# A hybrid pooling/HGRN2 trunk in float32: weights stored tile by tile, loaded a megabyte at a time

## The chip, the core and the metric

The kernel runs on one core of a Trainium2 chip. The metric is device time in microseconds (us), from launch to end, and lower is better. Batch 1, 256 tokens, model width 2048, two layers, all data float32. Each weight is read once, so some 570 MB come from HBM in every execution.

## The reference, cut to what matters

```python
def reference(x, c, ...):
    cond = silu(c)
    for layer in range(2):
        mod = cond @ w_ada[layer] + b_ada[layer]              # 2048 x 12288, a vector times a matrix
        sh_m, sc_m, g_m, sh_f, sc_f, g_f = split(mod, 6)
        h = rms_norm(x, norm_mix_gain[layer]) * (1 + sc_m) + sh_m
        if layer == 0: y = pool_mixer(h, pool_w[0], pool_scale[0])   # four 512 x 512 products
        else:          y = hgrn2_mixer(h, hgrn_w_in[0], ...)         # 2048 x 8192 and 2048 x 2048
        x = x + g_m * y
        h = rms_norm(x, norm_ffn_gain[layer]) * (1 + sc_f) + sh_f
        x = x + g_f * swiglu(h, w_ffn_in[layer], w_ffn_out[layer])   # 2048 x 11264 and 5632 x 2048
    return rms_norm(x, final_gain)
```

## The kernel before

**Dense weights.** Every dense product is split in two parts for accuracy. A weight pair is 2 x 128 rows by 512 columns (512 KB). SyncE loads it into one of four places of the ring `raw` (`load_w`, line 381). ScalarE rounds it into `w_hi` (line 940), VectorE takes the rest, `w_lo = raw - w_hi` (line 1273), and TensorE runs six matmuls for each of the pair's two steps of 128 rows (lines 613 to 615, twelve a pair). `w_hi` and `w_lo` have four places too (`SPL`). Three semaphores tie this together: `hi(n)` waits until pair n has arrived and until TensorE has used pair n - 4. The load of pair n waits for `lo_ready` to reach n - 3, that is for `w_lo` of pair n - 4. TensorE waits for `lo_ready`.

**Modulation.** The vector `mod` is made in units of 1024 columns, sixteen tiles of 128 rows by 1024 columns (512 KB) each. There are 24 units. The first seven (`HEAD`) come before the feed-forward part of layer 0, and there the ring of tiles has sixteen places (`ada` and `ada_head`). Within a unit of the head the first 6 to 9 tiles go to TensorE (`multiply_loads`, line 641), and the others are folded by VectorE (`fold`, lines 1319 and 1322), which before its last fold adds TensorE's part (line 1316). TensorE then sums over partitions (line 648, or 675 for gates), ScalarE takes the result (lines 966 to 973), and only then can TensorE begin the loads of the next unit, since `modp` is one buffer. The seventh unit (`MIX_F`) takes 512 columns from each of two sections.

The other 17 units (`BEHIND`) run beside the dense products, all sixteen tiles on VectorE, through four places (`ada`). Each has a span of steps in which its tiles fall due.

**Order.** There is no scheduler: SyncE, ScalarE and VectorE each walk through the same list of steps (one step is 128 rows of a weight chunk), and at each step do what falls due. SyncE at step s issues the raw load of that step's pair (when s is even) and then the modulation tiles due at s. ScalarE and VectorE do `hi` or `lo` of that pair at step s, then the evacuations and updates of earlier chunks, then the folds due at s. All queues are in order, so a wait in one instruction holds back all behind it. Layer 0's feed-forward input begins with chunks of only four steps (36 chunks), in whose second half VectorE also adds each chunk to a partial sum (`add_quarter`, line 1618), and TensorE waits for that before it reuses a `prod` buffer (`evacuated`).

The weights lie in HBM as given: a raw pair is 256 rows of 2048 bytes, a modulation tile 128 rows of 4096 bytes (the seventh and the eighth unit 256 rows of 2048).

Of the kernel before, what the change touches and what calls it, by code (L numbers as in the profile page):

```python
# [14 lines left out]
P = 128  # L15
CH = 512
# [23 lines left out]
    return [k for k in range(n) if first + k * (last - first + 1) // n == step]  # L40


def build(nc, x, c, norm_mix_gain, norm_ffn_gain, w_ada, b_ada, pool_w, pool_scale, hgrn_w_in,
          hgrn_w_out, hgrn_norm_gain, hgrn_lb, w_ffn_in, w_ffn_out, final_gain, out):
    D = x.shape[2]
    TB = x.shape[1] // P
    S = TB * P
    KD = D // P
    NCH = D // CH
    F = w_ffn_out.shape[1]  # L50
    KF = F // P
    NF = F // CH
    HG = CH // P
# [117 lines left out]
    with ctx:  # L171
# [3 lines left out]
        def sem(name):  # L175
            return ctx.enter_context(nc.semaphore(name))
# [87 lines left out]

        C_GMIX, C_GFFN, C_HGAIN, C_LB = KD, 3 * KD, 5 * KD, 6 * KD

        raw_loaded = [sem(f"raw_loaded{i}") for i in range(RAW)]
        ada_loaded = [sem(f"ada_loaded{i}") for i in range(ADA_HEAD)]
        ada_free = [sem(f"ada_free{i}") for i in range(ADA_HEAD)]
        params_loaded = sem("params_loaded")  # L270
# [81 lines left out]
        def ada_buffer(slot):  # L352
            return ada[:, slot] if slot < ADA else ada_head[:, slot - ADA]

        def ada_arrived(eng, n):
            slot, before = ada_slot(n)
            eng.wait_ge(ada_loaded[slot], 16 * (before + 1))

        def ada_used(eng, n):
# [12 lines left out]
        @block.sync  # L372
        def _(sp):
            t = Tally()

            def load_w(src):
                n = t.get("raw")
                slot = n % RAW
                if n >= RAW:
                    sp.wait_ge(lo_ready, n - RAW + 1)  # L380
                sp.dma_start(raw[:, slot], src.rearrange("(a p) n -> p a n", p=P)).then_inc(raw_loaded[slot], 16)  # L381
                t.tick("raw")

            def load_ada():
                u, k = t.get("ada") // KD, t.get("ada") % KD
                layer, section, half = UNITS[u]
                mixed = section == MIX_F
                at = SH_F * D + half * CH if mixed else section * D + half * UW
                if k == ADA and not in_columns(u):
                    n = rows_before(u)  # L390
                    if n > 1:
                        sp.wait_ge(unit_summed, 2 * (n - 1))
                    for r in range(2):
                        row = 64 * (n % 2) + 32 * r
                        col = at + r * (D if mixed else CH)
                        sp.dma_start(bias[row:row + 1, :], b_ada[layer:layer + 1, col:col + CH]).then_inc(bias_loaded[n % 2], 16)
                slot, before = ada_slot(t.get("ada"))
                if before:
                    sp.wait_ge(ada_free[slot], before)
                block = w_ada[layer, k * P:(k + 1) * P]  # L400
                if mixed:
                    block = block[:, SH_F * D:(SC_F + 1) * D].rearrange("p (a d) -> p a d", a=2)[:, :, half * CH:(half + 1) * CH]
                    into = ada_buffer(slot).rearrange("p (a n) -> p a n", a=2)
                    sp.dma_start(into, block).then_inc(ada_loaded[slot], 16)  # L404
                else:
                    sp.dma_start(ada_buffer(slot), block[:, at:at + UW]).then_inc(ada_loaded[slot], 16)  # L406
                t.tick("ada")

            def load_unit(first=0, last=KD):
                for _ in range(first, last):  # L410
                    load_ada()

            def load_chunk(src, at, first, n, loaded=0):
                for s in range(n):
                    if s % 2 == 0 and s >= loaded:
                        k = first + s
                        load_w(src[k * P:(k + 2) * P, at:at + CH])
                    for span in SPAN.values():
                        for _ in due(t.get("step"), KD, *span):
                            load_ada()  # L420
                    t.tick("step")

            at = 0
            for src in (c, norm_mix_gain, norm_ffn_gain, hgrn_norm_gain, hgrn_lb):
                n = src.shape[0] * KD
                sp.dma_start(rows[at:at + n, :], src.rearrange("l (k p) -> (l k) p", p=P)).then_inc(params_loaded, 16)
                at += n
            load_unit(0, ADA)
            for n, section in enumerate((SH_M, SH_F)):
                sp.dma_start(brows[2 * n * KD:2 * (n + 1) * KD, :],  # L430
                             b_ada[0, section * D:(section + 2) * D].rearrange("(k p) -> k p", p=P)).then_inc(brows_loaded, 16)
            load_unit(ADA, KD)
            for tb in range(TB):
                sp.dma_start(xs[:, tb], x[0, tb * P:(tb + 1) * P, :]).then_inc(x_loaded, 16)
            load_unit()
            load_unit()
            load_chunk(pool_w[0, 0], 0, 0, HG)
            load_unit()
            load_chunk(pool_w[0, 1], 0, 0, HG)
            load_unit()  # L440
            load_chunk(pool_w[0, 2], 0, 0, HG)
            load_chunk(pool_w[0, 3], 0, 0, HG)
            sp.dma_start(pscale[:, :, :].rearrange("p a n -> p (a n)"),
                         pool_scale[0:1, :].to_broadcast([P, D])).then_inc(pscale_loaded, 16)
            load_unit()
            for s in range(0, AHEAD, 2):
                load_w(w_ffn_in[0, s * P:(s + 2) * P, 0:CH])
            load_unit()

            def load_ffn_in(layer):  # L450
                for first, n in ((0, HALF), (HALF, HALF)) if layer else ((0, HG), (HG, HG), (HALF, HALF)):
                    for j in range(NA):
                        for o in range(2):
                            load_chunk(w_ffn_in[layer], o * F + j * CH, first, n, 0 if layer or first or j or o else AHEAD)
                for j in range(NA, NF):
                    for o in range(2):
                        load_chunk(w_ffn_in[layer], o * F + j * CH, 0, KD)

            load_ffn_in(0)
            for n in range(NCH):  # L460
                load_chunk(w_ffn_out[0], n * CH, 0, KF)
            load_chunk(hgrn_w_in[0], D, 0, KD)
            load_chunk(hgrn_w_in[0], 0, 0, KD)
            for i in range(NCH):
                load_chunk(hgrn_w_in[0], i * CH + 2 * D, 0, KD)
                load_chunk(hgrn_w_in[0], i * CH + 3 * D, 0, KD)
                if i + 1 < NCH:
                    load_chunk(hgrn_w_in[0], i * CH + (D + CH), 0, KD)
                    load_chunk(hgrn_w_in[0], i * CH + CH, 0, KD)
            for first, n in ((0, WFIRST), (WFIRST, HG)):  # L470
                for half in range(2):
                    load_chunk(hgrn_w_out[0], half * CH, first, n)
            for n in range(2, NCH):
                load_chunk(hgrn_w_out[0], n * CH, 0, KD)
            load_ffn_in(1)
            for n in range(NCH):
                if n == NCH - 1:
                    assert t.get("ada") == KD * len(UNITS)
                    for slot in range(2):
                        ada_used(sp, t.get("ada") - ADA + slot)  # L480
                    sp.dma_start(fgain, final_gain.rearrange("(a n) -> a n", a=1).to_broadcast([P, D])).then_inc(fgain_loaded, 16)
                load_chunk(w_ffn_out[1], n * CH, 0, KF)
            last = D - CH
            sp.wait_ge(y_ready, 1)
            sp.dma_start(out[0, 0:P, last:], xs[:, 0, last:]).then_inc(stored, 16)
            sp.wait_ge(y_block, 1)
            sp.dma_start(out[0, 0:P, 0:last], xs[:, 0, 0:last]).then_inc(stored, 16)
            sp.wait_ge(y_ready, 2)
            sp.dma_start(out[0, P:S, CH:], xs[:, 1, CH:]).then_inc(stored, 16)
            sp.wait_ge(y_block, 2)  # L490
            sp.dma_start(out[0, P:S, 0:CH], xs[:, 1, 0:CH]).then_inc(stored, 16)
            sp.wait_ge(stored, 16 * 4)
# [438 lines left out]
        def _(act):  # L931
            t = Tally()

            def hi():
                n = t.get("pair")
                r, slot = n % RAW, n % SPL
                act.wait_ge(raw_loaded[r], 16 * (n // RAW + 1))
                if n >= SPL:
                    act.wait_ge(w_used, n - SPL + 1)
                act.activation(w_hi[:, slot], raw[:, r], ACT.Copy).then_inc(hi_ready, 1)  # L940
# [325 lines left out]
        def _(dve):  # L1266
# [636 lines left out]

_NAMES = ["x", "c", "norm_mix_gain", "norm_ffn_gain", "w_ada", "b_ada", "pool_w", "pool_scale", "hgrn_w_in",
          "hgrn_w_out", "hgrn_norm_gain", "hgrn_lb", "w_ffn_in", "w_ffn_out", "final_gain"]


# [14 lines left out]
```

## Time and profile before

| | us |
|---|---|
| median of 3 runs | 2180.79 (2180.61 to 2182.24) |
| the profiled execution | 2180.74 |
| its span, first to last instruction | 2179.0 |
| TensorE busy in the span | 2129.1 (98%) |
| VectorE busy | 1641.3 (75%) |
| ScalarE busy | 998.5 (46%) |
| moved by DMA | 574.34 MB, mean 264 GB/s |

The span is read in three parts. The head, up to 180 us, makes the first seven modulation units and the pooling mixer, and there the DMA queue is full all the time. From 180 to about 400 us the first chunks of the feed-forward part run with modulation tiles beside them, and VectorE is busy nearly all the time. The rest is dense products with TensorE at 97 to 100% of nearly every slice. "PE" is TensorE, "PEld" its weight loads, "DVE" VectorE, "ACT" ScalarE, "SPq" the queue of SyncE.

### The profile page before, as it was taken

To read this page: it belongs to the slowest core of one execution; us is meant where nothing else is said; L and a number is where in the kernel's file an instruction comes from. 1 tells how busy PE (TensorE), PEld (TensorE's weight loads), DVE (VectorE), ACT (ScalarE), POOL (GpSimd) and SP (SyncE) were. 2 spreads that over 40 slices of the span, in tenths; PEclk is the share of its full clock that TensorE was granted. 3 is DMA by queue.
4 is the path that set the end of the run, shared out by engine and by line. 5 is a ranking of instruction groups with operands and counts; after the bars stand their busy time and mean duration, and the time that the engine had idled before them with its cause. 6 is when DMAs were issued, how large, how long until landed. Compare 5 with 4: busy or idle time off the path is not lost.

```text
span 2179.0 us, 24643 instructions
## 1 busy us (share of the span) xinstructions
PE 2129.1 (98%) x9513; PEld 1724.2 (79%) x9513; DVE 1641.3 (75%) x1685; ACT 998.5 (46%) x1116; POOL 21.0 (1%) x89
## 2 busy tenths in 40 slices
PE   7999999999999999999999999999999999999997
PEld 3556887888888888878888888878888888888886
DVE  5778899999988887769787887677755665546644
ACT  3224544444444344455655556544454444444433
POOL 1000000000000000020000000000000000000000
PEclk9999999999999999999999999999999999999999
DMA  9999998999899998757666765578866666658663
GB/s 375 406 400 356 334 349 290 323 319 316 313 337 328 348 331 289 260 175 232 220 197 216 224 196 163 186 281 303 280 185 189 185 182 189 192 188 299 234 216 135
DMA packets 250353, 574.34 MB, mean 264 GB/s; under 512 B 17558, under 2 KB 17750, under 8 KB 249724
## 3 DMA queue, kind: packets, MB, share of 16 engines
q1 hardware_dynamic: 250236, 572.77, 77.2%
q8 instruction: 75, 1.23, 0.2%
q14 instruction: 42, 0.34, 0.0%
HBM read 570.60 MB, written 2.10 MB: 263 GB/s over the span
## 4 chain that ended last, share of the span: by engine, by line
PE 89%; DVE 4%; SPq 3%; DMA 2%; issue 2%; ACT 0%; ACTq 0%; DVEq 0%
PE prod L613 28%; PE prod L615 27%; PE prod L614 27%; PE small L684 1%; DVE acc L1322 1%; SPq L406 1%; DMA ada_head<-in_w_ada 1%; PE modp L641 1%; PE small L856 1%; SPq L404 1%; DMA pscale<-in_pool_scale 1%; SPq L381 1%; PE small L831 0%; PE modp L675 0%; DVE feat L1322 0%
## 5 line engine op out<-in xcount | busy, mean ns | idle before, releaser
L940 ACT ACTIVATE w_hi<-raw 128x1024 fp32r<-128x1024 f32 x696 | 736.4, 1061 | 992.8 <-PE prod L615 892.7
L1273 DVE TENSOR_TENSOR w_lo<-raw,w_hi 128x1024 fp32r<-128x1024 f32 x696 | 848.8, 1223 | 419.7 <-ACT w_hi L940 418.1
L613 PE MATMUL prod<-w_hi,h_hi 128*128 128x512 f32 x2072 | 819.3, 395 | 4.8 <-issue 1.9
L615 PE MATMUL prod<-w_hi,h_lo 128*128 128x512 f32 x2072 | 808.9, 390 | 0.0
L614 PE MATMUL prod<-w_lo,h_hi 128*128 128x512 f32 x2072 | 808.5, 390 | 0.0
L613 PEld LDWEIGHTS prod<-w_hi,h_hi 128*128 128x128 f32 x2072 | 390.3, 188 | 86.6 <-issue 3.2
L615 PEld LDWEIGHTS prod<-w_hi,h_lo 128*128 128x128 f32 x2072 | 389.7, 188 | 81.7
L614 PEld LDWEIGHTS prod<-w_lo,h_hi 128*128 128x128 f32 x2072 | 390.3, 188 | 78.7 <-issue 1.0
L1322 DVE SCALAR_TENSOR_TENSOR acc<-ada,cond,acc 128x1024 f32<-128x1024 f32 x255 | 326.4, 1280 | 0.4
L613 PE MATMUL prod<-w_hi,g_hi 128*128 128x512 f32 x688 | 269.1, 391 | 0.0
L615 PE MATMUL prod<-w_hi,g_lo 128*128 128x512 f32 x688 | 268.0, 390 | 0.0
L614 PE MATMUL prod<-w_lo,g_hi 128*128 128x512 f32 x688 | 267.9, 389 | 0.0
L614 PEld LDWEIGHTS prod<-w_lo,g_hi 128*128 128x128 f32 x688 | 129.2, 188 | 27.2 <-issue 0.5
L613 PEld LDWEIGHTS prod<-w_hi,g_hi 128*128 128x128 f32 x688 | 129.2, 188 | 27.2 <-issue 0.5
L615 PEld LDWEIGHTS prod<-w_hi,g_lo 128*128 128x128 f32 x688 | 129.2, 188 | 26.7
L641 PE MATMUL modp<-ada,cond_rows 128*128 128x512 f32 x112 | 56.4, 662 | 12.3 <-DMA brows<-in_b_ada 6.8
L641 PEld LDWEIGHTS modp<-ada,cond_rows 128*128 128x128 f32 x112 | 23.5, 215 | 41.9 <-issue 39.0
L684 PE MATMUL small<-ident,tok 128*128 128x128 f32 x272 | 37.4, 282 | 7.0 <-issue 4.8
L684 PEld LDWEIGHTS small<-ident,tok 128*128 128x128 f32 x272 | 32.8, 145 | 13.8 <-issue 6.9
L641 PE MATMUL modp<-ada_head,cond_rows 128*128 128x512 f32 x96 | 42.3, 592 | 0.0
L1322 DVE SCALAR_TENSOR_TENSOR acc<-ada_head,cond,acc 128x1024 f32<-128x1024 f32 x29 | 37.2, 1284 | 3.7 <-DMA ada_head<-in_w_ada 1.4
L1022 ACT ACTIVATE feat<-small,mod,gain 128x256 f32<-128x256 f32 x48 | 23.4, 563 | 29.2 <-PE small L684 26.7
(196 smaller groups left out, 1052.5 us busy)
## 6 DMA issues: line engine op xcount, KB each, us to landing
raw<-in_w_ffn_in SPq DMA_DIRECT2D x352, 512.0 KB, 4.6
ada<-in_w_ada SPq DMA_DIRECT2D x300, 512.0 KB, 6.2
raw<-in_w_ffn_out SPq DMA_DIRECT2D x176, 512.0 KB, 4.7
raw<-in_hgrn_w_in SPq DMA_DIRECT2D x128, 512.0 KB, 3.9
ada_head<-in_w_ada SPq DMA_DIRECT2D x84, 512.0 KB, 14.8
raw<-in_hgrn_w_out SPq DMA_DIRECT2D x32, 512.0 KB, 3.8
raw<-in_pool_w SPq DMA_DIRECT2D x8, 512.0 KB, 15.6
xs<-in_x SPq DMA_DIRECT2D x2, 1024.0 KB, 17.0
```

The lines of the kernel that those rows point to most:

```text
L381: sp.dma_start(raw[:, slot], src.rearrange("(a p) n -> p a n", p=P)).then_inc(raw_loaded[slot], 16)
L404: sp.dma_start(into, block).then_inc(ada_loaded[slot], 16)
L406: sp.dma_start(ada_buffer(slot), block[:, at:at + UW]).then_inc(ada_loaded[slot], 16)
L613: pe.matmul(o, hi[:, k, ts], wh, start=(begin and s == 0), stop=False)
L614: pe.matmul(o, hi[:, k, ts], wl, start=False, stop=False)
L615: mm = pe.matmul(o, lo[:, k, ts], wh, start=False, stop=(end and s == n - 1))
L641: mm = pe.matmul(modp[:, o], cond_rows[:, k], ada_buffer(slot)[:, o * CH:(o + 1) * CH], start=(k == 0), stop=(in_columns(u) and k == n_row ...
L684: mm = pe.transpose(small[half][:, o:o + P], block_of(tb, 2 * half + j), ident[:, :])
L940: act.activation(w_hi[:, slot], raw[:, r], ACT.Copy).then_inc(hi_ready, 1)
L1022: ins = act.activation(feat[:, half, j], small[half][:, j * S:(j + 1) * S], ACT.Identity, bias=shifts[:, k:k + 1], scale=gains[:, k:k + 1])
L1273: dve.tensor_tensor(w_lo[:, slot], raw[:, r], w_hi[:, slot], ALU.subtract).then_inc(lo_ready, 1)
L1322: ins = dve.scalar_tensor_tensor(a, ada_buffer(slot), cond[:, k:k + 1], a, ALU.mult, ALU.add)
```

## The change

Three things, all about how weights lie in HBM and how they are loaded. No arithmetic of the program changes.

- Before the launch, dense weights are stored tile by tile (`weight_tiles`): a tile is 512 rows by 512 columns, laid so that each of 128 partitions has its four row pieces, 8192 bytes, in one run. The tile is 1 MB in one piece. The modulation weights are stored as pairs of tiles (`modulation_tiles`), 8192 bytes a partition, and the mixed units lie ready in an array of their own.
- `load_w` loads such a tile, two pairs, with one DMA into two neighbouring places of `raw`. It waits for `lo_ready` to reach n - 2 (n even), that is for `w_lo` of pair n - 3. `raw_loaded` has two semaphores instead of four, and `hi` of either pair waits for the whole tile.
- In the head `load_ada` loads two modulation tiles with one DMA, once both places are free, and every user of either tile waits for both. Behind the head it still loads one tile at a time, in rows of 4096 bytes.

```diff
+def weight_tiles(w):
+
+    lead, (K, N) = w.shape[:-2], w.shape[-2:]
+    n = len(lead)
+    w = w.reshape(*lead, K // (4 * P), 4, P, N // CH, CH)
+    return w.transpose(*range(n), n + 3, n, n + 2, n + 1, n + 4).reshape(*lead, N // CH, K // (4 * P), P, 4 * CH)
+
+
+def modulation_tiles(w):
+
+    L, D, _ = w.shape
+    sections = w.reshape(L, D // (2 * P), 2, P, 6, 2, D // 2).transpose(0, 4, 5, 1, 3, 2, 6)
+    mixed = w[0, :, 3 * D:5 * D].reshape(D // (2 * P), 2, P, 2, D // CH, CH)[:, :, :, :, 0:2].transpose(4, 0, 2, 1, 3, 5)
+    return sections, mixed.reshape(2, D // (2 * P), P, 2, 2 * CH)
...
-        raw_loaded = [sem(f"raw_loaded{i}") for i in range(RAW)]
+        raw_loaded = [sem(f"raw_loaded{i}") for i in range(RAW // 2)]
...
         def ada_arrived(eng, n):
+
             slot, before = ada_slot(n)
+            if n < len(HEAD) * KD:
+                slot -= slot % 2
+            elif slot % 2:
+                before -= len(HEAD) * KD // ADA_HEAD
             eng.wait_ge(ada_loaded[slot], 16 * (before + 1))
...
                 if n >= RAW:
-                    sp.wait_ge(lo_ready, n - RAW + 1)
-                sp.dma_start(raw[:, slot], src.rearrange("(a p) n -> p a n", p=P)).then_inc(raw_loaded[slot], 16)
-                t.tick("raw")
+                    sp.wait_ge(lo_ready, n - RAW + 2)
+                sp.dma_start(raw[:, slot:slot + 2].rearrange("p b a n -> p (b a n)"), src).then_inc(raw_loaded[slot // 2], 16)
+                t.tick("raw", 2)
...
                 slot, before = ada_slot(t.get("ada"))
-                if before:
+                tiles = ada_mixed[half] if mixed else ada_sections[layer, section, half]
+                if u >= len(HEAD):
                     sp.wait_ge(ada_free[slot], before)
-                block = w_ada[layer, k * P:(k + 1) * P]
...
-                    sp.dma_start(ada_buffer(slot), block[:, at:at + UW]).then_inc(ada_loaded[slot], 16)
+                    sp.dma_start(ada_buffer(slot), tiles[k // 2, :, k % 2]).then_inc(ada_loaded[slot], 16)
+                elif k % 2 == 0:
+                    for tile in range(2 if before else 0):
+                        sp.wait_ge(ada_free[slot + tile], before)
+                    sp.dma_start(ada_pair(slot).rearrange("p k n -> p (k n)"),
+                                 tiles[k // 2].rearrange("p k n -> p (k n)")).then_inc(ada_loaded[slot], 16)
                 t.tick("ada")
...
-                    if s % 2 == 0 and s >= loaded:
+                    if s % 4 == 0 and s >= loaded:
                         k = first + s
-                        load_w(src[k * P:(k + 2) * P, at:at + CH])
+                        load_w(src[at // CH, k // 4])
...
-                act.wait_ge(raw_loaded[r], 16 * (n // RAW + 1))
+                act.wait_ge(raw_loaded[r // 2], 16 * (n // RAW + 1))
```

## Rows read from the trace of the kernel before

**Rows 1.** The page: span, busy time of the engines.
```profile
span 2179.0 us, 24643 instructions
...
PE 2129.1 (98%) x9513; PEld 1724.2 (79%) x9513; DVE 1641.3 (75%) x1685; ACT 998.5 (46%) x1116; POOL 21.0 (1%) x89
```

**Rows 2.** Stretches: length, busy of five engines, PEclk, DMA share, GB/s.
```profile
12.00:16.00 4.00, 4.00 (x7) 1.70 (x7) 0.00 (x0) 0.00 (x0) 0.00 (x0) 1.00 1.03 412
26.00:28.00 2.00, 0.00 (x0) 0.00 (x0) 1.91 (x2) 0.00 (x0) 0.00 (x0) 1.00 1.04 430
26.00:31.00 5.00, 1.69 (x8) 1.59 (x8) 4.87 (x5) 0.00 (x0) 0.00 (x0) 0.74 1.00 415
...
146.00:154.00 8.00, 8.00 (x37) 6.64 (x36) 5.85 (x6) 0.00 (x0) 0.00 (x0) 1.00 1.04 387
...
310.00:335.00 25.00, 23.21 (x100) 18.21 (x99) 24.80 (x24) 9.38 (x9) 0.00 (x0) 1.00 0.83 281
360.00:378.00 18.00, 16.87 (x77) 13.36 (x77) 17.93 (x18) 8.07 (x10) 0.00 (x0) 1.00 0.77 271
```

**Rows 3.** Who waited for whom: total us, times, longest.
```profile
SPq L381 <- DVE w_lo L1273: 1513.4, 677, 16.8
...
ACT w_hi L940 <- PE prod L615: 892.7, 573, 4.4
...
PE prod L613 <- DVE part_value L1618: 1.8, 2, 1.6
...
PE prod L613 <- DVE part_gate L1618: 1.1, 2, 0.7
```

**Rows 4.** Timeline, the head: start, us, engine, line, operation [idle before].
```profile
16.41 0.76 DVE L1319 TENSOR_SCALAR acc<-ada_head,cond 128x1024 f32<-128x1024 f32 x1 [7.12 <-DMA ada_head<-in_w_ada]
17.62 9.62 DVE L1322 SCALAR_TENSOR_TENSOR acc<-ada_head,cond,acc 128x1024 f32<-128x1024 f32 x7 [0.45 <-DMA ada_head<-in_w_ada]
...
125.53 1.02 ACT L966 ACTIVATE gate<-modp 128x1024 f32<-128x1024 f32 x1 [23.02 <-PE modp L675]
...
129.40 2.81 PE L641 MATMUL modp<-ada,cond_rows 128*128 128x512 f32 x6 [3.90 <-DMA ada<-in_w_ada]
```

**Rows 5.** Timeline, one pair in the steady state, on ScalarE, VectorE and SyncE.
```profile
719.15 1.06 ACT L940 ACTIVATE w_hi<-raw 128x1024 fp32r<-128x1024 f32 x1 [1.66 <-PE prod L615]
721.88 1.06 ACT L940 ACTIVATE w_hi<-raw 128x1024 fp32r<-128x1024 f32 x1 [1.66 <-PE prod L615]
...
720.25 1.23 DVE L1273 TENSOR_TENSOR w_lo<-raw,w_hi 128x1024 fp32r<-128x1024 f32 x1 [0.30 <-ACT w_hi L940]
...
721.50 0.37 SPq L381 DMA_DIRECT2D raw<-in_w_ffn_out  x1
```

**Rows 6.** The tile raw, 1000 to 1300 us: issue to landing of its loads.
```profile
DMA to landing us min/median/max: 3.6/3.9/6.8
```

**Rows 7.** DMA issues, 188 to 225 us: count, size, median us to landing.
```profile
raw<-in_w_ffn_in SPq DMA_DIRECT2D x13, 512.0 KB, 8.3
```

**Rows 8.** Timeline of VectorE, 258 to 358 us.
```profile
264.92 1.22 DVE L1273 TENSOR_TENSOR w_lo<-raw,w_hi 128x1024 fp32r<-128x1024 f32 x1
...
271.92 1.22 DVE L1273 TENSOR_TENSOR w_lo<-raw,w_hi 128x1024 fp32r<-128x1024 f32 x1
...
280.44 1.19 DVE L1273 TENSOR_TENSOR w_lo<-raw,w_hi 128x1024 fp32r<-128x1024 f32 x1
...
286.02 1.23 DVE L1273 TENSOR_TENSOR w_lo<-raw,w_hi 128x1024 fp32r<-128x1024 f32 x1 [1.00 <-ACT w_hi L940]
287.59 1.23 DVE L1618 TENSOR_TENSOR part_gate<-prod,part_gate 128x1024 f32<-128x1024 f32 x1 [0.34 <-PE prod L615]
...
334.94 1.18 DVE L1273 TENSOR_TENSOR w_lo<-raw,w_hi 128x1024 fp32r<-128x1024 f32 x1
...
339.44 2.35 DVE L1273 TENSOR_TENSOR w_lo<-raw,w_hi 128x1024 fp32r<-128x1024 f32 x2
...
346.19 1.22 DVE L1273 TENSOR_TENSOR w_lo<-raw,w_hi 128x1024 fp32r<-128x1024 f32 x1
```

More of the change, by code:

```diff
@@ L40, in due, with build @@
     return [k for k in range(n) if first + k * (last - first + 1) // n == step]
-def build(nc, x, c, norm_mix_gain, norm_ffn_gain, w_ada, b_ada, pool_w, pool_scale, hgrn_w_in,
+def weight_tiles(w):
[8 more added lines that the diff above has]
+    return sections, mixed.reshape(2, D // (2 * P), P, 2, 2 * CH)
+def build(nc, x, c, norm_mix_gain, norm_ffn_gain, ada_sections, ada_mixed, b_ada, pool_w, pool_scale, hgrn_w_in,
           hgrn_w_out, hgrn_norm_gain, hgrn_lb, w_ffn_in, w_ffn_out, final_gain, out):
@@ L49, in build @@
     NCH = D // CH
-    F = w_ffn_out.shape[1]
+    F = w_ffn_out.shape[2] * 4 * P
     KF = F // P
@@ L353, in ada_buffer, with ada_pair @@
             return ada[:, slot] if slot < ADA else ada_head[:, slot - ADA]
+        def ada_pair(slot):
+            return ada[:, slot:slot + 2] if slot < ADA else ada_head[:, slot - ADA:slot - ADA + 2]
         def ada_arrived(eng, n):
             slot, before = ada_slot(n)
+            if n < len(HEAD) * KD:
+                slot -= slot % 2
+            elif slot % 2:
+                before -= len(HEAD) * KD // ADA_HEAD
             eng.wait_ge(ada_loaded[slot], 16 * (before + 1))
@@ L397, in load_ada @@
                 slot, before = ada_slot(t.get("ada"))
-                if before:
+                tiles = ada_mixed[half] if mixed else ada_sections[layer, section, half]
+                if u >= len(HEAD):
                     sp.wait_ge(ada_free[slot], before)
-                block = w_ada[layer, k * P:(k + 1) * P]
[L401 to L405, printed above, removed]
-                    sp.dma_start(ada_buffer(slot), block[:, at:at + UW]).then_inc(ada_loaded[slot], 16)
+                    sp.dma_start(ada_buffer(slot), tiles[k // 2, :, k % 2]).then_inc(ada_loaded[slot], 16)
[4 more added lines that the diff above has]
+                                 tiles[k // 2].rearrange("p k n -> p (k n)")).then_inc(ada_loaded[slot], 16)
                 t.tick("ada")
@@ L445, in _ @@
             load_unit()
-            for s in range(0, AHEAD, 2):
-                load_w(w_ffn_in[0, s * P:(s + 2) * P, 0:CH])
+            for s in range(0, AHEAD, 4):
+                load_w(w_ffn_in[0, 0, s // 4])
             load_unit()
@@ L1905 @@
           "hgrn_w_out", "hgrn_norm_gain", "hgrn_lb", "w_ffn_in", "w_ffn_out", "final_gain"]
+_TILED = ("pool_w", "hgrn_w_in", "hgrn_w_out", "w_ffn_in", "w_ffn_out")
 def kernel(**inputs):
@@ L1912 @@
     nc = bacc.Bacc("TRN2", target_bir_lowering=False, num_devices=1, dynamic_dma_scratch_size=2048)
-    arrays, args = {}, []
+    placed = []
     for name in _NAMES:
         a = np.ascontiguousarray(inputs[name])
+        if name == "w_ada":
+            sections, mixed = modulation_tiles(a)
+            placed += [("ada_sections", sections), ("ada_mixed", mixed)]
+        else:
+            placed.append((name, weight_tiles(a) if name in _TILED else a))
+    arrays, args = {}, []
+    for name, a in placed:
+        a = np.ascontiguousarray(a)
         arrays[f"in_{name}"] = a
```

## The prediction

> **What bounds the kernel now.** I began with the page: span 2179.0 us, TensorE busy 2129.1 of it [rows 1]. So at most 50 us are idle, and whatever happens to DMA counts only where TensorE stands still for it. The profiled execution took 2180.74 us, 1.7 more than its span, and the median is 2180.79: the sum below is made against 2180.74 and holds for the median as it stands.
>
> Next I read stretches, to see where TensorE idles and what the DMA queue delivers [rows 2]. In the head the queue is always full, and its rate goes with the length of the rows it reads: 412 GB/s while modulation tiles (4096-byte rows) pass, 387 where the seventh unit (2048-byte rows) does, and 415 over the five microseconds that hold the two loads of x (8192-byte rows), with 430 in the best two of them. After the head TensorE is full except in two places: 310 to 335 us (1.8 idle) and 360 to 378 us (1.1 idle). The waits name the reason: lines 1618 of VectorE, 1.8 and 1.1 us [rows 3]. VectorE is busy 24.80 of 25 us and 17.93 of 18 us there [rows 2], so it is the bound of these places: each microsecond that VectorE loses between about 286 and 378 us is a microsecond of the end.
>
> Then the waits as a whole [rows 3]. ScalarE's `hi` stands 892.7 us for TensorE: dense weights are ahead of their use. SyncE stands 1513.4 us for `w_lo`: raw loads are late only because their place is taken. So the speed of a dense load is worth nothing by itself in most of the kernel; what the ring's two places do to its timing is the question.
>
> **The head: longer rows.** Six units of 16 tiles are 50.3 MB: 122.8 us at 410 GB/s, 121.3 at 415, 117.0 at 430. The seventh unit, 8.4 MB, goes from 21.7 us (387) to 20.2 or 19.5. The pooling weights, 4.2 MB in rows of 2048 bytes, go from 10.8 to 10.1 or 9.8, and the two first pairs of the feed-forward part save 0.2 to 0.3. The queue saves 3.9 us in all at 415 and 9.3 at 430. I take 415, which is the mean over whole transfers; the slice of 430 is two microseconds of the same five.
>
> How much of it reaches the end? The units are also tied by engines: reduce, take, then the next unit's loads on TensorE. Only one wait of TensorE on this path is for a modulation tile: 3.90 us before the loads of the sixth unit at 129.40 [rows 4]. Up to that tile the queue saves 1.2 us on 80 tiles and 0.7 on the pooling weights, 1.9 together. But the tile now comes with its neighbour, 1.28 us later (524 KB at 410 GB/s). So it is there at 129.40 - 1.9 + 1.28 = 128.8. What else would hold TensorE: the gate is taken by ScalarE at 125.53 + 1.02 = 126.55 [rows 4].
>
> That time moves too. In the first unit VectorE takes its first tile (the eighth) at 16.41 and the next at 17.62, when it lands [rows 4]. The eighth is the second of a pair, so it is not later; but the ninth is now half of a pair that lands 2.53 us (1 MB at 415) after the last, about 18.8 instead of 17.6. VectorE then folds without a break for 9.62 us, its last fold releases TensorE's sum, and the chain through the next units goes on from there: 1.2 us late. 126.55 becomes 127.7, still ahead of 128.8. So the head ends 0.6 us earlier. Bounds: 1.2 us later, if the pair's delay meets a place without cover (the cover is the 2.9 us between 126.55 and 129.40; if it is gone, the 1.2 counts), and 9.3 earlier, if the queue alone set the end. Fewer issues on SyncE count for nothing, since the queue is full behind them.
>
> **The ring in two places.** From one pair in the steady state [rows 5]: `hi` at 719.15, the next at 721.88, so a pair takes TensorE 2.72 us. `lo` runs 720.25 to 721.48, and SyncE issues the load for that place at 721.50. Before, the load of pair n + 4 is issued when `lo` of pair n ends. Now the load of pairs n + 4 and n + 5 is issued when `lo` of pair n + 1 ends, one pair later, and moves twice the bytes.
>
> The trace has no 1 MB raw load on a quiet queue. Below it lies the 512 KB load, 3.6 us at least and 3.9 in the median where no modulation tiles run [rows 6]; above it the same in a saturated queue, 8.3 [rows 7]. Doubling the bytes adds 2.53 - 1.35 = 1.2 us (1 MB at 415 less 512 KB at 387), so 4.8 on a quiet queue. I take 4.8, since SyncE now issues the raw tile ahead of the modulation tiles of its four steps; 6.0 is the upper value I carry, one modulation tile in front. The Trainium skill ("DMA: Bandwidth & Descriptors", section "Anatomy of one DMA") fits a DMA with 2.0 us plus bytes over 436 GB/s, which gives an estimate of 4.4 us for 1 MB; by it the cost below would be 2.0 instead of 3.5 us. That fit is for loads issued from GpSimd, and no run here yet shows a 1 MB load on its own.
>
> So between the end of `lo(n + 1)` and the start of `lo(n + 4)` there must be 4.8 + 1.06 (`hi`) + 0.1 (issue and hand-over) = 5.95 us. In the steady state there are 720.25 + 3 x 2.72 less 721.48, which is 6.9: it fits, at no cost, and `w_hi` holds four pairs ahead in any case. Over the stretch where VectorE has lagged and runs `lo` at its own pace I read the gaps for every even n [rows 8]:
>
> - 266.1 to 271.92: 5.8 us, short by 0.2, and the tile before it has the same gap. 0.4 us of lag in all.
> - 281.63 to 286.02: 4.4 us, short by 1.55, plus the 0.4 of lag. VectorE's 0.34 of idle at 287.59 takes some back. 1.6 us.
> - 336.12 to 340.6 (the second of the two at 339.44): 4.45, short by 1.5.
> - 340.7 to 346.19: 5.5, short by 0.4.
>
> 1.6 + 1.5 + 0.4 = 3.5 us, all before or between the two places where TensorE stands for VectorE, so they lengthen the run by 3.5. The bounds: 0.3, if a tile lands as fast as the quickest half of one does now, 3.6 us (the gap needed is then 4.75, and only the third gap is short of it by more than idle time gives back); and 9.5 with a landing of 6.0 (the gap needed is then 7.15: 1.35 twice, 2.75 less 0.34, 2.7 and 1.65). Later in the run such short gaps come too, but there TensorE no longer stands for VectorE, which is busy 1641.3 of 2179 us in all [rows 1]; I cost them at nothing, and if that cover is gone each costs 0.3 to 1.5.
>
> Moved with it: modulation tiles due at the first two of the four steps now wait behind a raw load that is issued one `lo` later. Their folds come after `lo(n)` on VectorE, at least 5.95 + 1.23 us after that release, and they land about 1.3 us behind the raw tile, at 6.1. No cost; what would wait is VectorE's queue. Longer rows also relieve the queue after the head, but TensorE doesn't wait for raw loads there [rows 3], so that is worth nothing.
>
> **The sum.** 2180.74 - 0.6 + 3.5 = 2183.6.
>
> **The rivals.**
> - *The head is a queue, and the stalls are absorbed.* The head ends earlier by most of what the queue saves, 3.9 to 9.3, and the ring costs nothing: 2171.4 to 2176.8, say 2174. For it: DMA is the only thing without any idle in the head. Against: one wait of TensorE for a tile, covered by an engine chain 2.9 us behind. The Trainium skill ("DMA: Bandwidth & Descriptors", section "Bandwidth") has 425 GB/s for 16 MB transfers; by that figure the six units would gain 4.3 us by themselves. The trace shows both 415 and 430 for such rows. Chance 0.20.
> - *The ring starves VectorE (slower).* At 250 to 400 us a raw tile queues behind modulation tiles, lands after 6.0, and VectorE, the bound there, loses 9.5: 2180.7 - 0.6 + 9.5 = 2189.6. It decides from a landing above 5.6 us. For it: the 8.3 us of a queue that is full [rows 7]. Against: between 310 and 335 us the queue delivers only 281 GB/s [rows 2], it isn't full. Chance 0.18.
> - *Nothing moves.* The pair's lateness eats the queue's gain and the landing is short enough: 2180 to 2181. This is also the case in which tiles or pairs do not bring what they say, rows of 8192 bytes being no faster than 4096. Chance 0.12.
> - The forecast, 0.50, with a range of its own of 2180 to 2187.
>
> **How the numbers follow.** 0.2% is 4.4 us and about what a measurement of this kernel can tell from no change: faster is below 2176.4, slower above 2185.2. Faster: 0.20. Slower: 0.18 and 0.05 from the forecast's upper end, 0.23. Same: 0.57. The range leaves out the lower half of the first rival and most of the second's upper part: 2174 to 2188.
>
> **What would show it.** In the trace of the changed kernel: the rate in the head 412 to 418 GB/s at all times; the sixth unit's first load at 128 to 129 us; the feed-forward part beginning 0.6 us earlier; a raw tile landing in 4.8 to 5.2 us where no modulation runs; VectorE waiting for ScalarE's `hi` near 286, 338 and 344; and TensorE's wait for line 1618 growing from 2.9 to 6 us. I am wrong in the head if the sixth unit starts at 127.7 or before, and in the ring if VectorE shows no new idle between 280 and 350 us, or if TensorE's waits for `lo` appear at all.

## The result, and the profile after

The changed kernel takes 2200.18 us (median of 4 runs, 2197.63 to 2201.99), the kernel before beside it 2180.7. The ratio is 1.0084, 95% interval 1.0072 to 1.0095: 18.3 us slower, give or take 2.5, and above the range. The profiled execution took 2201.99 us, its span is 2200.3.

The head first. Stretches of the changed kernel, 20 to 140 us (length, busy of five engines, PEclk, DMA share, GB/s):

```profile
20.00:60.00 40.00, 34.93 (x122) 21.88 (x121) 25.21 (x27) 14.91 (x36) 0.00 (x0) 0.87 1.01 419
60.00:100.00 40.00, 37.02 (x120) 21.59 (x119) 32.60 (x37) 11.05 (x21) 0.00 (x0) 0.91 1.01 420
100.00:140.00 40.00, 37.83 (x115) 20.16 (x115) 30.39 (x37) 8.29 (x15) 0.00 (x0) 1.00 1.01 419
```

The same three stretches of before have 410, 406 and 407 GB/s. Of the timeline of the changed head, the lines that answer to [rows 4], and between them (at 109.63) the start of the fifth unit on VectorE:

```profile
16.29 0.75 DVE L1343 TENSOR_SCALAR acc<-ada_head,cond 128x1024 f32<-128x1024 f32 x1 [7.01 <-DMA ada_head<-in_ada_sections]
18.70 9.61 DVE L1346 SCALAR_TENSOR_TENSOR acc<-ada_head,cond,acc 128x1024 f32<-128x1024 f32 x7 [1.66 <-DMA ada_head<-in_ada_sections]
...
109.63 0.76 DVE L1343 TENSOR_SCALAR acc<-ada_head,cond 128x1024 f32<-128x1024 f32 x1 [1.09 <-DMA ada_head<-in_ada_sections]
...
125.26 1.02 ACT L990 ACTIVATE gate<-modp 128x1024 f32<-128x1024 f32 x1 [21.29 <-PE modp L699]
...
127.13 3.24 PE L665 MATMUL modp<-ada,cond_rows 128*128 128x512 f32 x7 [1.91 <-DMA ada<-in_ada_sections]
```

The sixth unit begins at 127.13 and not at 129.40: the head became faster. Now the chain of work that ended last, from the page of the changed kernel, and under it the waits of the split (total us, times, longest), as in [rows 3]:

```profile
PE 73%; DVE 11%; DMA 10%; issue 4%; ACT 2%; SPq 0%; DVEq 0%; ACTq 0%
...
ACT w_hi L964 <- PE prod L639: 554.2, 373, 4.4
...
ACT w_hi L964 <- DMA raw<-in_w_ffn_in: 343.7, 114, 6.3
ACT w_hi L964 <- DMA raw<-in_w_ffn_out: 106.3, 38, 4.6
...
PE prod L637 <- DVE w_lo L1297: 7.2, 8, 1.6
```

Before, the chain ran 89% through TensorE, 4% VectorE and 2% DMA; ScalarE waited 80.6 us, 52 times, for a raw tile of the feed-forward input weights; and TensorE never waited for `lo`. Now it does, eight times by this row and again before weight loads. Where? Stretches of the changed kernel behind the head, in the columns of [rows 2]:

```profile
250.00:380.00 130.00, 120.22 (x517) 95.20 (x516) 118.43 (x120) 54.45 (x63) 0.00 (x0) 0.99 0.84 308
380.00:660.00 280.00, 272.68 (x1219) 220.48 (x1219) 253.77 (x243) 116.71 (x125) 0.00 (x0) 1.00 0.83 306
660.00:920.00 260.00, 259.79 (x1151) 213.43 (x1150) 212.51 (x197) 104.88 (x113) 0.00 (x0) 1.00 0.87 322
```

And the same of the kernel before:

```profile
250.00:380.00 130.00, 127.08 (x568) 103.29 (x567) 124.22 (x127) 60.08 (x65) 0.00 (x0) 1.00 0.88 316
380.00:660.00 280.00, 279.98 (x1272) 230.86 (x1271) 262.99 (x251) 126.11 (x131) 0.00 (x0) 1.00 0.91 323
660.00:920.00 260.00, 260.00 (x1149) 213.92 (x1148) 210.36 (x193) 106.67 (x111) 0.00 (x0) 1.00 0.89 312
```

TensorE is busy 6.9 us less in the first stretch and 7.3 less in the second, and VectorE, which before was 96% and 94% busy there, stands still more as well. From 660 us on the two are alike. Idle time alone doesn't add up to the loss: over the whole span TensorE is idle 12.1 us more (62.0 against 49.9) and busy 9.2 us more (2138.3 against 2129.1) for the same 9513 matmuls. Where the 9.2 lie isn't settled. A small part shows in the granted clock. The kernel before has it at 1.00 from 360 to 378 us; the changed one stands still for 2.4 us there and has 0.91:

```profile
360.00:378.00 18.00, 15.56 (x65) 12.55 (x65) 17.30 (x20) 8.49 (x14) 0.00 (x0) 0.91 0.81 285
```

The clock's own record has 3.4 us at the lower level (1.2 GHz) there, which is worth 1.7 us at most.

The best view of where time goes is a difference of two timelines: the start of `lo` of pair n after, less the start of the same before. Worked out from the starts of lines 1297 and 1273:

```
pair n                    8     30     38     50     70    120    160    280    500    695
before, starts at us  176.2  236.2  262.6  293.8  352.0  497.1  609.7  953.4 1619.2 2158.2
after, later by us     -3.0    2.4    0.1    5.9    8.4   14.7   24.2   20.6   21.2   21.2
```

So the head gives 3.0 us, the stretch up to 352 us takes 11.4 (3.1 of it before pair 38, with which the gaps of [rows 8] begin, and 8.3 from there), and the one up to some 610 us takes 12.8 more, net of what comes back behind it. After 950 us next to nothing is lost, with the same ring. One place of the losing stretch, in the changed kernel, on ScalarE, VectorE and SyncE:

```profile
290.31 2.01 ACT L964 ACTIVATE w_hi<-raw 128x1024 fp32r<-128x1024 f32 x2 [3.66 <-DMA raw<-in_w_ffn_in]
298.60 2.01 ACT L964 ACTIVATE w_hi<-raw 128x1024 fp32r<-128x1024 f32 x2 [6.29 <-DMA raw<-in_w_ffn_in]
...
286.54 2.35 DVE L1297 TENSOR_TENSOR w_lo<-raw,w_hi 128x1024 fp32r<-128x1024 f32 x2
291.40 1.22 DVE L1297 TENSOR_TENSOR w_lo<-raw,w_hi 128x1024 fp32r<-128x1024 f32 x1 [2.50 <-ACT w_hi L964]
...
285.52 0.33 SPq L405 DMA_DIRECT2D raw<-in_w_ffn_in  x1
285.90 1.64 SPq L425 DMA_DIRECT2D ada<-in_ada_sections  x3
288.92 0.33 SPq L405 DMA_DIRECT2D raw<-in_w_ffn_in  x1
```

The two `lo` at 286.54 end at 288.89, SyncE issues the next megabyte at 288.92, and `hi` can start at 298.60: a landing of 9.7 us, behind three modulation tiles issued since 285.90. That is twice the 4.8 of the sum. The median in such stretches, from the DMA issues of the changed kernel, first 250 to 380 us, then 380 to 660, then 1000 to 1300 where few tiles compete:

```profile
raw<-in_w_ffn_in SPq DMA_DIRECT2D x21, 1024.0 KB, 6.2
...
raw<-in_w_ffn_in SPq DMA_DIRECT2D x47, 1024.0 KB, 5.7
...
raw<-in_hgrn_w_in SPq DMA_DIRECT2D x48, 1024.0 KB, 4.8
```

### The profile page after: what moved, and what is told of

Same layout as the page of the kernel before. It is cut to its first block, busy times and chain, and to the rows that moved or that the text cites. A ratio compares the mean times of both kernels' runs of the same rounds, so it can differ in the third digit from the quotient of the medians.

```text
span 2200.3 us, 24287 instructions
## 1 busy us (share of the span) xinstructions
PE 2138.3 (97%) x9513; PEld 1724.8 (78%) x9513; DVE 1638.4 (74%) x1685; ACT 987.5 (45%) x1116; POOL 23.6 (1%) x89
## 4 chain that ended last, share of the span: by engine, by line
PE 73%; DVE 11%; DMA 10%; issue 4%; ACT 2%; SPq 0%; DVEq 0%; ACTq 0%
PE prod L637 22%; PE prod L639 22%; PE prod L638 22%; DMA raw<-in_w_ffn_in 7%; DVE acc L1346 4%; DVE w_lo L1297 3%; PE modp L665 2%; ACT w_hi L964 1%; DMA ada<-in_ada_sections 1%; PE small L708 1%; DMA raw<-in_w_ffn_out 1%; PE small L880 1%; PE modp L672 1%; DMA ada_head<-in_ada_sections 1%; PE modp L699 1%
## 5 line engine op out<-in xcount | busy, mean ns | idle before, releaser
L964 ACT ACTIVATE w_hi<-raw 128x1024 fp32r<-128x1024 f32 x696 | 726.8, 1058 | 1029.1 <-PE prod L639 554.2
L665 PEld LDWEIGHTS modp<-ada_head,cond_rows 128*128 128x128 f32 x96 | 18.2, 190 | 23.0 <-issue 23.0
```

What stands on the lines that cost most here:

```text
L665: mm = pe.matmul(modp[:, o], cond_rows[:, k], ada_buffer(slot)[:, o * CH:(o + 1) * CH], start=(k == 0), stop=(in_columns(u) and k == n_row ...
```

## The experiments

The theory (A): the ring of two places frees a place one pair later, and the megabyte that then starts lands late because modulation tiles are in flight in front of it; VectorE, which has no time to spare between 250 and 650 us, waits for it. Rival B: the new layout or the modulation tiles lose the time. The rivals C to F stand in the expectations.

**Undo the megabyte loads.** The new layout and the new head stay; a load carries one pair into a place of its own.

```
-                    sp.wait_ge(lo_ready, n - RAW + 2)
-                sp.dma_start(raw[:, slot:slot + 2]..., src).then_inc(raw_loaded[slot // 2], 16)
+                    sp.wait_ge(lo_ready, n - RAW + 1)
+                sp.dma_start(raw[:, slot]..., src).then_inc(raw_loaded[slot], 16)
```

> The changed kernel with one part undone: a dense weight load carries one pair of tiles (512 KB, 4 KB a row, still out of the new layout) into a place of its own and is issued when the split of the pair three before the next one has ended, as in the kernel before. Layout and head stay as changed. Theory A (the ring of two places starves the split: a place comes free one pair later and a megabyte lands 1.2 us later, behind modulation tiles in flight): the loss goes altogether and the 1.85 us that the head gained stay, 2178.8 us, 2177.5 to 2180.5; ScalarE's waits for a raw tile of the feed-forward input weights fall from 344 us to the 80 us of before or less. Theory B (the loss comes from the layout or from the modulation tiles, not from the ring): the time stays at 2197 to 2203 us.

Measured: 2178.66 us, ratio 0.9988, interval 0.9979 to 0.9997. The waits of the split in this kernel:

```profile
ACT w_hi L964 <- PE prod L639: 886.6, 571, 4.4
...
ACT w_hi L964 <- DMA raw<-in_w_ffn_in: 91.4, 54, 3.5
```

The whole loss is the ring's; layout and head keep their gain. The wait for raw tiles is near the 81 us of before, slightly over it. And the loads land no sooner than the megabytes, here from 250 to 380 us:

```profile
raw<-in_w_ffn_in SPq DMA_DIRECT2D x43, 512.0 KB, 6.2
```

Worked out for the even pairs from 80 to 170, the load that `hi` waits for has landed 5.97 us after the `lo` that releases it, in the mean, in this kernel and in the changed one alike. But in the changed one that `lo` is one pair later. `hi` starts 1.05 us after the landing with pair loads (median), and 0.02 us after it in the changed kernel. So what a load takes is the same, and the time in which it may land is one pair shorter.

**Undo the modulation part.** The modulation tiles lie and are loaded as before; dense weights as changed.

> The changed kernel with the other part undone: the modulation tiles lie and are loaded as in the kernel before (one at a time, 2 or 4 KB a row, out of the original array), the dense weights keep the new layout, the megabyte loads and the two places. Theory A: the loss of the ring stays and the head's gain goes, 2202 us, 2200 to 2205. Theory B for the modulation tiles (their new layout or their twos are what loses time behind the head): 2179 to 2184 us.

Measured: 2200.62 us, ratio 1.0090, interval 1.0075 to 1.0105. In the head the rate is 410 GB/s again. Rival B falls from this side too. The loss is as large without the new modulation tiles, and the head's gain doesn't show against it: the time is 0.4 us above the changed kernel by the medians and 1.3 by the ratios, where 2 were expected, and all of this is inside the intervals.

**Two halves.** Both halves of a tile are issued when the megabyte is, with a semaphore each.

```
+                for b in range(2):
+                    sp.dma_start(raw[:, slot + b]..., src[:, b * 2 * CH:(b + 1) * 2 * CH]).then_inc(raw_loaded[slot + b], 16)
```

> The changed kernel with the megabyte load split into two loads of 512 KB with a semaphore each, both issued at the same moment as the megabyte load is now (two pairs free). Only the arrival of the first pair moves: in the quiet parts of the kernel before 512 KB landed in 3.6 us where a megabyte takes 4.8. Theory A with the size as its main part: the first split of a tile starts up to 1.2 us earlier and most of the 21 us go, 2180 to 2188 us. Theory A with the late release as its main part (the place freed one pair later, the 1.2 to 3 us that modulation tiles in flight add being the same for both sizes): 2189 to 2197 us. Theory B: 2200 us.

Measured: 2188.35 us, ratio 1.0032, interval 1.0019 to 1.0045. This parts the loss. From pair loads to two halves only the release is later: 9.7 us (9.6 by the ratios). From two halves to the megabyte the first split also waits for the second half: 11.8 us (11.3 by the ratios). By the intervals each share is uncertain by 3 to 4 us, so neither is "the main part". By the starts and landings of the loads, the first half lands 5.0 us after its issue in the median between 380 and 620 us, the whole megabyte 5.7.

The 9.7 us have a second way that the theory leaves out. VectorE of this kernel also waits for modulation tiles:

```profile
DVE acc L1348 <- DMA ada<-in_ada_sections: 36.4, 46, 2.5
```

With pair loads it doesn't wait for one behind the head. The likely reason, argued and not shown: SyncE issues in order, so a later release holds back the modulation loads behind the raw load as well. In the changed kernel, where VectorE stands for late raw tiles instead, such waits come to 0.6 us. How much of the 9.7 goes this way no run separates.

**Pair loads, but the split waits for both.**

```
+                if n % 2 == 0:
+                    act.wait_ge(raw_loaded[r], 16 * (n // RAW + 1))
+                    act.wait_ge(raw_loaded[r + 1], 16 * (n // RAW + 1))
```

> The kernel with pair loads (each issued when its own place is free, new layout, new head) in which ScalarE's first split of every two pairs also waits for the second pair's load. So the release that counts is as late as with two places, but what is loaded after it is 512 KB and not a megabyte. Theory A with the size as its main part: as with the two halves, 2180 to 2188 us. Theory A with the late release as its main part: 2189 to 2197 us. Theory B: 2200 us.

Measured: 2205.26 us, ratio 1.0108, interval 1.0091 to 1.0125: worse than the changed kernel, outside every value I had given. The DMA issues of this kernel, 380 to 660 us, count, size and median landing:

```profile
raw<-in_w_ffn_in SPq DMA_DIRECT2D x94, 512.0 KB, 5.6
ada<-in_ada_sections SPq DMA_DIRECT2D x70, 512.0 KB, 6.6
```

Half the bytes land hardly sooner: 5.6 us against 5.7 for the megabyte. In this stretch what stands in front of a load moves its landing more than its size does (the two halves showed 0.7 us for the size), so a shorter load doesn't buy the late release back. Why it is 5 us worse still stays open. It isn't a later issue or landing: for the even pairs from 80 to 170 the second load of two is issued 0.03 us after its release in the median and has landed 5.73 us after it in the mean, against 5.97 of the changed kernel. By the starts of `lo`, pair 160 is 21.5 us late here and 24.2 in the changed kernel; the excess comes behind it, with TensorE idle for 3.7 us from 660 to 920 us against 0.2.

**Thin modulation loads**, in the changed kernel and in the one before.

```
-                    sp.dma_start(ada_buffer(slot), tiles[k // 2, :, k % 2])...
+                    sp.dma_start(ada_buffer(slot)[:, 0:64], tiles[k // 2, :, k % 2, 0:64])...
```

> The changed kernel, in which each modulation load behind the head (272 of them) brings only the first 64 of its 1024 columns; every wait, fold and semaphore stays, so those modulation rows are computed from stale data. It takes modulation tiles out of the way of the raw tiles and nothing else. Theory A (a megabyte lands too late because modulation tiles are in flight before it): raw tiles land in 4.8 us as in the quiet stretches, the loss goes, 2176 to 2182 us, within 0.15% of the same edit made to the kernel before. Rival C (the late release is enough for the loss, VectorE being full, whatever is in flight): 2188 to 2200 us.

> The same edit made to the kernel before: each modulation load behind the head brings 64 columns (64 of the first half for the mixed unit), all else stays; those modulation rows come from stale data. Both theories: the old ring had room for the landing it had, 2176 to 2181 us. It is the measure for the thin loads in the changed kernel.

Measured: 2185.22 us and 2180.33 us (ratios 1.0014, interval 1.0005 to 1.0024, and 0.9998, interval 0.9989 to 1.0007). The issues of the changed kernel so edited, 380 to 660 us, and a stretch of it:

```profile
raw<-in_w_ffn_in SPq DMA_DIRECT2D x49, 1024.0 KB, 4.8
...
380.00:660.00 280.00, 277.26 (x1257) 227.58 (x1256) 261.44 (x249) 119.70 (x128) 0.00 (x0) 1.00 0.56 195
```

With the DMA share down from 0.83 to 0.56 the megabyte lands in 4.8 us, and of the distance of 19.5 us between the two kernels 4.9 are left (by the ratios 3.5 of 18.3). So three quarters of it or more come from the tiles in flight. Both expectations missed: the rest isn't nothing, as theory A had it, and isn't what rival C wanted. Late release and whole tile together cost 4.9 at a landing of 4.8 us, some 7 if the head's 2 are added; the 9.7 and 11.8 us of the two halves are what they cost behind tiles in flight. The starts of `lo`, against the kernel before, say where the rest lies:

```
pair n                    8     30     38     50     70    120    160    280    500    695
thin loads, later by   -2.6   -2.6   -2.6   -1.1    0.4    4.3    6.5    2.9    5.4    5.3
```

From pair 38 to pair 70, the stretch for which the prediction worked out 3.5 us at this very landing, 3.0 are lost. The other 4.9 are lost behind it.

**Short folds**, in the changed kernel and in the one before.

```
-                    ins = dve.scalar_tensor_tensor(a, ada_buffer(slot), cond[:, k:k + 1], a, ALU.mult, ALU.add)
+                    few = UW if u < len(HEAD) else 64
+                    ins = dve.scalar_tensor_tensor(a[:, 0:few], ada_buffer(slot)[:, 0:few], cond[:, k:k + 1], a[:, 0:few], ...)
```

> The changed kernel, in which each fold of a modulation tile behind the head works on the first 64 of 1024 columns (some 0.1 to 0.2 us in place of 1.28), so that VectorE has about 1.1 us a fold to spare, 300 us in all; the loads stay whole, and those modulation rows are wrong. Theory A as a matter of cover (the wait for a raw tile costs time because VectorE is full there): the raw tiles land as late as before, 5.5 to 6.5 us, yet no more than a third of the 21 us is left, 2176 to 2186 us. Rival D (the ring's own loop, release, landing, high part, low part, is longer than three pairs on TensorE, so it binds whatever VectorE does): 2188 to 2200 us.

> The same short folds in the kernel before. Both theories: TensorE is the bound there, VectorE is not, 2175 to 2181 us. It is the measure for the short folds in the changed kernel.

Measured: 2177.29 us and 2179.24 us (ratios 0.9979, interval 0.9970 to 0.9989, and 0.9987, interval 0.9977 to 0.9997). In the changed kernel so edited, the issues and the stretch from 380 to 660 us:

```profile
raw<-in_w_ffn_in SPq DMA_DIRECT2D x50, 1024.0 KB, 6.0
...
380.00:660.00 280.00, 280.00 (x1273) 230.57 (x1272) 198.50 (x256) 127.17 (x134) 0.00 (x0) 1.00 0.87 323
```

The raw tiles land as late as ever (6.0 us), ScalarE still waits for them, yet TensorE is busy all 280 us: VectorE now has 81 us to spare in these 280 and catches up. No loss is left that these runs could tell: the changed kernel is the faster one by 2.0 us (1.7 by the ratios), as much as the head's gain, give or take 2 to 3. Rival D falls. A late raw tile costs time only because VectorE is full.

**A third place**, paid for with two modulation places, and pair loads under the same cut as its measure.

```
-    RAW = 4
+    RAW = 6
-    ADA, ADA_HEAD = 4, 16
+    ADA, ADA_HEAD = 2, 14
```

> The changed kernel with three places of a megabyte in the raw ring in place of two; the room comes from the modulation ring, which falls from four tiles to two (and from 16 to 14 in the head). A raw tile can then be issued two pairs before the first high part that needs it is due after the last one, one whole tile ahead. Theory A: the split no longer waits for a raw tile (the 344 us of ScalarE's waits fall below those of the kernel before, 81 us); what is lost, if anything, is the modulation ring's, and it is lost by the pair loads with two modulation tiles as well: within 0.2% of that kernel, or faster. Against four modulation tiles and pair loads (2178.7 us): 2178 to 2195 us. Rival E (a megabyte at a time costs something that no place in the ring gives back): slower than the pair loads with two modulation tiles by 5 us or more.

> The kernel with pair loads (new layout, new head), with the modulation ring cut from four tiles to two, and from 16 to 14 in the head. It is the measure for the three places. SyncE then waits longer for a free modulation place and holds the raw loads behind it, and VectorE waits for modulation tiles that land late: 2178 to 2195 us.

Measured: 2286.11 us (1.0476, interval 1.0461 to 1.0492) and 2250.08 us (1.0309, interval 1.0292 to 1.0326). SyncE's waits for the place of a modulation tile, first with three places, then with pair loads:

```profile
SPq L425 <- DVE acc L1346: 664.9, 220, 8.0
...
SPq L425 <- DVE acc L1346: 515.2, 197, 6.8
```

In the changed kernel this row has 21.4 us. SyncE issues in order: every raw load now stands behind a wait for a fold, and a free third place doesn't help a load that hasn't been reached. Both times lie far above the 2178 to 2195 us that I expected, and the pair misses its aim. It shows that the room for a third place can't be had from the modulation ring. Three places are 36 us slower than the pair loads under the same cut, so by its wording rival E holds. SyncE's waits are longer too (664.9 against 515.2 us), but no run shows that they make up the 36, so this pair doesn't refute rival E. Whether three places with four modulation tiles would do stays open.

**The head one tile at a time**, 4 KB rows out of the new layout, dense weights in pair loads.

> The kernel with pair loads, in which the modulation tiles of the head are loaded one at a time too (512 KB, 4 KB a row, out of the new layout) and not in twos. If the head's rate of 419 GB/s in place of 410 comes from the rows of 8 KB, it falls back to 410 and the time to 2179.5 to 2182 us, as in the kernel before; if it comes from the layout (tiles that lie together), the rate stays at 419 and a unit's first tiles land earlier than in twos: 2177.5 to 2179 us.

Measured: 2181.75 us, ratio 0.9994, interval 0.9985 to 1.0004. The head of this kernel:

```profile
20.00:60.00 40.00, 35.38 (x127) 21.35 (x126) 25.39 (x29) 14.93 (x36) 0.00 (x0) 0.91 1.02 410
```

The rate is back at 410, so the head's gain doesn't come from tiles that lie together. But a load also went from 1 MB back to 512 KB, and the time can't part the two. The records of the single packets can. A packet is one row here: from 20 to 140 us one of 2048, 4096 and 8192 bytes takes 88, 163 and 316 ns in the mean in the kernel before, 163 and 315 of the latter two in this one, and 315 for 8192 bytes in the changed one, 1 MB loads and 512 KB loads alike. Two packets of 4096 bytes take 11 ns more than one of 8192. So it is the row. In time the two versions differ by 1.3 us (0.9994 to 0.9988), with intervals that overlap; the rate is the firm part.

**Megabytes only behind the dense stretch.** Pair loads up to pair 272, the changed kernel's loads from there.

> The kernel with pair loads up to the start of the recurrent part (the first 272 pairs, where most modulation tiles are loaded), and from there on the changed kernel's way: a megabyte at a time into two places, 424 pairs in 212 loads, issued when two pairs are free. Theory A with its place (the ring of two places loses only where the DMA queue is full and VectorE is full): these loads cost nothing, the time is that of the pair loads throughout, 2178.7 us, 2177 to 2181. Rival F (the late release costs a little at every tile, wherever it is): above 2183 us.

Measured: 2178.02 us, ratio 0.9984, interval 0.9975 to 0.9993. The 212 late-released megabyte loads cost nothing that can be told, rival F falls, and this is, with the pair loads, the version that beats both kernels, by 0.16% against the one before and 1.0% against the changed one. Its own waits for raw tiles are 192.8 us for the feed-forward input weights, twice those of the pair loads, and cost nothing either: there VectorE has room.

## Why the prediction was wrong, step by step

**What bounds the kernel.** Right: "each microsecond that VectorE loses" counts, but I bounded it to 286 to 378 us because only there TensorE stood still. TensorE standing still marks where VectorE's margin is already zero. Where it is small, as from 380 to 660 us with VectorE 94% busy, the losses of the new ring first eat the margin and then count as well: 12.8 us behind 352 us, costed at nothing. The prediction's own sum would have warned. In the trace of the kernel before, 11 of the 50 gaps from pair 70 to pair 170 are too short for a landing of 4.8 us, by 8.8 us together, and 22 are too short for 5.7, by 24.0. In that stretch the changed kernel falls back by 14.4 and the one with thin loads by 4.4. The bound began earlier than 286 us, too: from 250 to 286 us TensorE stood still for 2.7 us after the change and not at all before. The short folds show that this margin is the matter.

**The head.** Rate: 415 in place of 410 taken, 419 to 420 in place of 406 to 410 measured. By the means of the three stretches (419.3 and 407.7) the 80 tiles save 2.8 us and not 1.2, an estimate, and 129.40 - 2.8 - 0.7 + 1.28 gives 127.2 for the sixth unit. The first unit went as foreseen, the second tile on VectorE at 18.70 (foreseen 18.8). The 1.2 us of lateness I carried through to 127.7 by the chain of units; it reached only the fourth. The takes of the first four units come 1.0 to 1.5 us later than before (the fourth at 103.79 against 102.34), but the fifth unit starts on VectorE when its tile lands, and that is 109.63 against 111.20. So the take of the gate is at 125.26, 0.3 earlier than before, and the sixth unit at 127.13, not 128.8. The head ends 2 to 3 us earlier (3.0 by the starts of pair 8; 2.0 by the short folds; 3.0 by the pair loads' medians, 2.6 by their ratio), where I had 0.6.

**The ring's condition.** The gap "landing + 1.06 + 0.1" and the way of adding up held where the landing was right: with thin loads, at 4.8 us, 3.0 lost for 3.5 worked out. With the landing of 6.2 us that the changed kernel has in this stretch, the gap needed is 7.4, and the five gaps of [rows 8] are short by 1.6, 1.6, 3.0 less 0.34, 2.95 and 1.9: 10.7 us. Measured from pair 38 to pair 70: 8.3. Another 3.1 are lost between pairs 8 and 38, for which no gap was costed; that the two together, 11.4, come near 10.7 is chance.

**The landing is the first of the two steps that failed.** I took 4.8 us, from loads of the quiet stretch [rows 6]. As the landing on a quiet queue it is exact: 4.8 in the median of 1000 to 1300 us. (The estimate of 4.4 by the Trainium skill, "DMA: Bandwidth & Descriptors", section "Anatomy of one DMA", is 0.4 too short here.) But the losing stretch isn't quiet. The issues of the kernel before, 250 to 380 us and 380 to 660 us, had it all along:

```profile
raw<-in_w_ffn_in SPq DMA_DIRECT2D x43, 512.0 KB, 5.4
...
raw<-in_w_ffn_in SPq DMA_DIRECT2D x100, 512.0 KB, 5.8
```

The second step is the cover behind 378 us, put at nothing. It is the larger of the two: with the right landing alone the sum would have been some 2191 us. A landing must be read in the stretch where it is used. Two arguments kept me from it. "SyncE now issues the raw tile ahead of the modulation tiles of its four steps" is true of the four steps to come and says nothing of those just issued, as 285.90 shows. And against the rival I held 281 GB/s, "it isn't full": beside it [rows 2] have a DMA share of 0.83, and the stretch just before it had

```profile
286.00:310.00 24.00, 24.00 (x107) 19.59 (x106) 23.46 (x25) 8.68 (x9) 0.00 (x0) 1.00 1.01 377
```

a share of 1.01 in the kernel before. GB/s says what is moved; the landing follows the share. In the kernel before, a 512 KB load lands in 3.9 us (median) at a share of 0.69 (1000 to 1300 us), in 5.4 at 0.88 and in 5.8 at 0.91.

**The rivals.** The ring that starves VectorE was the right one, "a landing above 5.6 us" included; its price of 9.5 us was too low because it was taken at 6.0 us and for one stretch only. Range and forecast fell with the same two steps: the landing (3.5 instead of 8.3 us from pair 38 to pair 70, and 3.1 before it) and the cover behind pair 70 (0 instead of 12.8). The head was 1.4 to 2.4 us off the other way.

## What to carry to other kernels

A ring in fewer and larger places has two prices, the later release and the longer landing; both are paid out of the gap between the last release and the next use, and that gap is to be compared with the landing measured in the same stretch, tiles in flight and all. Whether a missed gap costs anything is the margin of the engine that waits: with VectorE 94% busy 14.4 us were lost on gaps short by 24.0, with it 71% busy nothing. Take the larger rows where a queue is the bound (the head), and keep the finer grain where an engine without margin eats from the ring. The Trainium skill's rule of 1 MiB or more to a DMA ("DMA: Bandwidth & Descriptors", section "Rules for kernel authors") is one for bandwidth. The head doesn't test it, since its gain (419 against 410 GB/s) comes from the length of the row; and the ring, where release and landing count and not the rate, is 1% slower for following it than with pair loads.

## What the runs showed of the hardware

- Loads with 8 KB to a row run at 419 GB/s where 4 KB rows give 410 from the old layout (with dense weights as changed) and 410 from the new one, with the queue full in all three. A packet of 2048, 4096 and 8192 bytes takes 88, 163 and 315 ns there, whatever the size of the load. "DMA: Bandwidth & Descriptors" of the Trainium skill, section "Bandwidth", has 425 for 16 MB; these are loads of 1 MB in a row.
- Behind modulation tiles 512 KB landed in 5.6 us and 1 MB in 5.7 (medians of one stretch, two kernels), while on a quiet queue the same two take 3.9 and 4.8. The share of the DMA engines was 0.87 and 0.83 there. I had expected the size to show in both. Issued at the same moment, the first 512 KB of two land 0.7 us before a whole megabyte (5.0 and 5.7).
